# A hybrid trunk's first layer: exponentials moved to VectorE, a shorter parameter chain on GpSimd, and two steps moved forward in their queues

## The reference, cut to what matters

```
sh, sc, gt = split(silu(c) @ w_mod + b_mod, 3)          # the modulation
h = rms_norm(tokens, g) * (1 + sc) + sh                 # the prologue, for all 1280 tokens
u, v, g_a, xs, g_b = split(h @ w_in)                     # 5 parts of 512 columns
y_a = u * (w_s @ layer_norm(v) + b_s) * silu(g_a)        # chunked gMLP
dt  = exp(log_dt);  mag = exp(lam_re * dt)               # S5 discretization, 128 x 32 numbers
lb  = mag * (cos(lam_im * dt) + i sin(lam_im * dt))
f   = (lb - 1) / lam;   bb = f * b                       # then powers lb^1 .. lb^8
y_b = S5 scan of xs, both directions, from lb, bb, c     # then GELU, GLU, silu(g_b)
x   = x + gt * ([y_a, y_b] @ w_out)
```

## Time and profile before

| | us |
|---|---|
| median of 3 runs | 1297.3 |
| the profiled execution, own time | 1298.54 |
| its span | 1296.7 |
| TensorE busy, share of the span | 1221.9, 94% |
| VectorE / ScalarE / GpSimd busy | 814.5 / 518.7 / 499.6 |
| front: VectorE's `den` steps end | 11.3 |
| front: VectorE adds the squares, from | 12.2 |
| front: sums' input ready | 20.1 |
| front: norm refined (VectorE) | 24.7 |
| front: its rows spread and copied (ScalarE) | 27.1 |
| front: second modulation column block (TensorE) | 33.3 |
| front: first `v` operand complete (VectorE) | 35.6 |
| front: TensorE at the fourth modulation block | 48.4 |

### The profile page before, as it was taken

One profiled execution on the slowest core, in us unless ns is written; L12 is line 12 of the kernel. 1 busy time (PEld: TensorE's weight loads), 2 busy tenths in 40 slices (PEclk: granted clock), 3 DMA queues, 4 the chain that ended last, 5 costly groups with the idle time before them and its releaser, 6 DMA issues.

```text
span 1296.7 us, 20964 instructions
## 1 busy us (share of the span) xinstructions
PE 1221.9 (94%) x8450; PEld 1077.2 (83%) x8450; DVE 814.5 (63%) x1381; ACT 518.7 (40%) x968; POOL 499.6 (39%) x447
## 2 busy tenths in 40 slices
PE   3889899999999899999999999999999999999997
PEld 2888778887888849999999998877788888887997
DVE  4569647989916263146475899448876777765125
ACT  3633454220015331133524432147566666665012
POOL 5850000000000003331112112139999999998332
PEclk9998999999999899999999999999999999999998
DMA  9832677325431952113111122330000000000402
GB/s 336 318 106 91 171 216 247 131 87 200 168 107 61 333 216 86 34 42 135 53 34 34 33 74 82 106 98 9 9 17 9 17 11 15 17 9 9 163 29 103
DMA packets 89232, 130.09 MB, mean 100 GB/s; under 512 B 12944, under 2 KB 59408, under 8 KB 88336
## 3 DMA queue, kind: packets, MB, share of 16 engines
q1 hardware_dynamic: 79312, 113.96, 26.4%
q10 hardware_dynamic: 9824, 14.80, 3.4%
HBM read 97.81 MB, written 30.93 MB: 99 GB/s over the span
## 4 chain that ended last, share of the span: by engine, by line
PE 75%; DVE 7%; POOL 7%; DMA 6%; ACT 2%; issue 2%; SPq 1%; ACTq 0%; POOLq 0%; DVEq 0%
PE ps L1804 9%; PE ps L1806 9%; PE ps L1805 9%; PE ps L1815 5%; PE ps L1816 5%; PE ps L1817 5%; DVE region_d L1096 3%; PE ps L2063 3%; PE ps L2097 3%; PE ps L2098 3%; PE ps L2099 3%; POOL shared L553 3%; PE ps L2083 3%; PE ps L2086 3%; PE ps L2085 3%; PE ps L2084 2%
## 5 line engine op out<-in xcount | busy, mean ns | idle before, releaser
L1804 PE MATMUL ps<-w_hi,a_hi 128*128 128x256 f32 x896 | 257.2, 287 | 6.2 <-DVE b_lo L1152 2.4
L1805 PE MATMUL ps<-w_lo,a_hi 128*128 128x256 f32 x896 | 255.1, 285 | 0.0
L678 POOL TENSOR_TENSOR region_b<-region_b,region_d 128x256 f32<-128x256 f32 x40 | 29.8, 751 | 480.9 <-DVE region_d L1480 480.9
L1806 PE MATMUL ps<-w_hi,c_lo 128*128 128x256 f32 x736 | 209.2, 284 | 0.0
L1804 PEld LDWEIGHTS ps<-w_hi,a_hi 128*128 128x128 f32 x896 | 173.7, 194 | 9.0 <-issue 4.5
L1805 PEld LDWEIGHTS ps<-w_lo,a_hi 128*128 128x128 f32 x896 | 173.6, 194 | 0.0
L671 POOL TENSOR_TENSOR w_lo<-weight_ring,w_hi 128x2048 fp32r<-128x2048 f32 x16 | 74.1, 4631 | 200.1 <-ACT w_hi L726 200.1
L1576 DVE TENSOR_REDUCE small<-ps 128x1 f32<-128x1280 f32 x64 | 95.3, 1489 | 75.3 <-PE ps L2063 75.3
L1806 PEld LDWEIGHTS ps<-w_hi,c_lo 128*128 128x128 f32 x736 | 142.3, 193 | 0.0
L1815 PE MATMUL ps<-a_hi,w_hi 128*128 128x512 f32 (+1 forms) x384 | 138.0, 359 | 1.3 <-ACT region_d L726 1.3
L1816 PE MATMUL ps<-b_lo,w_hi 128*128 128x512 f32 (+1 forms) x384 | 136.0, 354 | 0.0
(11 more groups left out here) (234 smaller groups left out, 2940.4 us busy)
## 6 DMA issues: line engine op xcount, KB each, us to landing
weight_ring<-in_w_mod SPq DMA_DIRECT2D x10, 2048.0 KB, 9.2
weight_ring<-in_we_in SPq DMA_DIRECT2D x10, 1024.0 KB, 6.3
weight_ring<-in_wo_in SPq DMA_DIRECT2D x10, 1024.0 KB, 5.2
weight_ring<-cop_t_scratch SPq DMA_DIRECT2D x4, 1536.0 KB, 7.9
region_c<-in_w_mod SPq DMA_DIRECT2D x2, 2048.0 KB, 14.7
bop_scratch<-region_d ACTq DMA_DIRECT2D x16, 256.0 KB, 2.0
cop_t_scratch<-region_d SPq DMA_DIRECT2D x8, 512.0 KB, 7.5
weight_ring<-bop_scratch SPq DMA_DIRECT2D x2, 2048.0 KB, 10.4
```

What stands on the lines that cost most here:

```text
L1804: te.matmul(o, th, wh[:, k], start=first and k == 0, stop=False)
L1805: te.matmul(o, th, wl[:, k], start=False, stop=False)
L1806: last = te.matmul(o, tl, wh[:, k], start=False, stop=stop and k == KT - 1)
```

## The change

Four things are changed.

1. The two exponentials leave GpSimd. VectorE makes them with a new `exp_` of 16 steps, in which multiply and add are fused into `scalar_tensor_tensor`. The first stands right after `den`, before the squares are added; the second right after the squares are added, before the norm. The semaphore `s_exp` tells GpSimd of each; `s_den_ok` is gone.
2. GpSimd's chain starts at the angle, after the first exponential. It drops a copy, selects between sine and cosine with one difference instead of two masks, writes `lr` and `li` where the powers need them, and makes real and imaginary part of a power product in one operation of twice the width (four operations per doubling instead of six).
3. The first modulation block (`mods(0)`, `mod_cols(0)` on TensorE, `mod_row(0)` on ScalarE) stands ahead of the norm's sums. On ScalarE the rounding of the first `v` weights stands ahead of the copy of the norm's rows. The first four k now go through `gained`, `gained_round` and `gained_rest` like the others; for tokens 256 to 767 VectorE takes `gained` and `gained_rest` of one k in turn.
4. SyncE loads the second `xs` weights ahead of `cop_out(0)`.

```diff
@@ SyncE
+            ring_load("xs", 1)
             cop_out(0)
-            ring_load("xs", 1)
             kt_out(0)
@@ GpSimd
-            pool.wait_ge(s_ld_par, 16 * 3)
-            exp_(dt, ldt)
-            tt(xe, lamr, dt, ALU.mult)
-            exp_(mg, xe)
+            lr, li = LP[:, 1, 0], LP[:, 1, 1]
+            step(g.memset(LP[:, 0, 0], 1.0))
+            step(g.memset(LP[:, 0, 1], 0.0))
+            pool.wait_ge(s_exp, 1)
             tt(th, lami, dt, ALU.mult)
...
-            tt(sn, s_, even, ALU.mult)
-            tt(t1, c_, odd, ALU.mult)
-            tt(sn, sn, t1, ALU.add)
-            tt(cn, c_, even, ALU.mult)
-            tt(t1, s_, odd, ALU.mult)
-            tt(cn, cn, t1, ALU.add)
+            tt(t1, c_, s_, ALU.subtract)
+            tt(t1, t1, odd, ALU.mult)
+            tt(sn, s_, t1, ALU.add)
+            tt(cn, c_, t1, ALU.subtract)
             tt(sn, sn, sin_sign, ALU.mult)
             tt(cn, cn, cos_sign, ALU.mult)
+            pool.wait_ge(s_exp, 2)
...
             for m in (1, 2, 4):
...
+                A, O = LP[:, 1:m + 1], LP[:, m + 1:2 * m + 1]
+                M_ = [LP[:, m, r].unsqueeze(1).unsqueeze(1).broadcast_to([P, m, 2, G]) for r in range(2)]
+                tmp = ctmp[:, 0:2 * m * G].rearrange("p (m r g) -> p m r g", r=2, g=G)
+                tt(O, A, M_[0], ALU.mult)
+                tt(tmp, A, M_[1], ALU.mult)
+                tt(O[:, :, 0], O[:, :, 0], tmp[:, :, 1], ALU.subtract)
+                tt(O[:, :, 1], O[:, :, 1], tmp[:, :, 0], ALU.add)
@@ ScalarE
+            mod_row(0)
             act.wait_ge(s_ss_mm, 1)
             act.wait_ge(s_consts, 2)
             a.activation(rstd[:, 0:6], sums, ACT.Sqrt, bias=epsc, scale=1.0 / D).then_inc(s_rt, 1)
+            weights_round(("v", 0))
             act.wait_ge(s_bc_mm, 1)
             copy(rstd_rows[:, 0:T01], rows01).then_inc(s_bc_ok, 1)
-            weights_round(("v", 0))
-            mod_row(0)
             mod_row(1)
-            h_round(0)
-            h_round(1)
+            gained_round(0, range(4), 0)
+            gained_round(1, range(4), 4)
@@ VectorE
-            v.reciprocal(den, den).then_inc(s_den_ok, 1)
+            step(v.reciprocal(den, den))
+            def exp_(o, xin):
...
+                ts(x_, xin, -87.0, ALU.max, 88.0, ALU.min)
+                ts(k_, x_, 1.0 / math.log(2.0), ALU.mult, ROUND, ALU.add)
+                ts(k_, k_, -ROUND, ALU.add)
+                st(r_, k_, -LN2_HI, x_, ALU.mult, ALU.add)
+                st(r_, k_, -LN2_LO, r_, ALU.mult, ALU.add)
+                ts(e_, r_, 1.0 / 5040, ALU.mult)
+                for q in (720.0, 120.0, 24.0, 6.0, 2.0, 1.0):
+                    st(e_, e_, 1.0 / q, r_, ALU.add, ALU.mult)
+                ts(k_, k_, 127.0, ALU.add, 2.0 ** 23, ALU.mult)
+                cp(p_, k_)
+                st(e_, e_, 1.0, p_.bitcast(F32), ALU.add, ALU.mult)
+                v.scalar_tensor_tensor(out=o, in0=xin, scalar=-87.0, in1=e_, op0=ALU.is_ge, op1=ALU.mult).then_inc(s_exp, 1)
+            exp_(dt, ldt)
+            dve.wait_ge(s_exp, 1)
+            tt(xe, lamr, dt, ALU.mult)
...
             v.tensor_tensor(XQ[:, 0, 0:T01], XQ[:, 0, 0:T01], XQ[:, 4, 0:T01], ALU.add).then_inc(s_pre, 1)
+            exp_(mg, xe)
...
-            scaled(0)
-            scaled(1)
             weights_rest(("v", 0))
+            dve.wait_ge(s_bc_ok, 1)
             half_evac(0)
-            h_rest(0)
-            h_rest(1)
+            gained(0, range(4))
+            gained_rest(0, range(4), 0)
+            for k in range(4):
+                gained(1, (k,))
+                gained_rest(1, (k,), 4 + k)
@@ TensorE
+            mods(0)
+            mod_cols(0)
             pe.wait_ge(s_pre, 1)
             for t in range(6):
                 last = te.matmul(sums[:, t:t + 1], XQ[:, 0, P * t:P * t + P], onec, start=True, stop=True)
             last.then_inc(s_ss_mm, 1)
             rstd_across(0)
-            mods(0)
-            mod_cols(0)
             mods(1)
```

More of the change, by code:

```diff
@@ L258, in build @@
             sem("mod_mm"), sem("mod_ok"), sem("sq"), sem("rt_req"), sem("rt_ok"))
[L259 to L260 removed]
+        s_pre, s_bc_mm, s_bc_ok, s_v_mm, s_v_ev, s_ss_mm, s_z2 = (
+            sem("pre"), sem("bc_mm"), sem("bc_ok"), sem("v_mm"), sem("v_ev"), sem("ss_mm"), sem("z2"))
         s_vn_ok, s_vg_ok, s_bl_ok, s_bl_tr, s_bl_ev, s_cl_ok = (
@@ L559, in cp @@
                 step(g.tensor_copy(o, a))
[L561 to L578, removed]
             def halved(o, xin):
@@ L598, in _ @@
             ts(kf, kf, -ROUND, ALU.add)
-            cp(rr, th)
-            for q in PIO2:
+            for i, q in enumerate(PIO2):
                 ts(t1, kf, -q, ALU.mult)
-                tt(rr, rr, t1, ALU.add)
+                tt(rr, rr if i else th, t1, ALU.add)
             tt(r2, rr, rr, ALU.mult)
@@ L608, in _ @@
             tt(s_, s_, rr, ALU.mult)
+            ts(c_, r2, -1.0 / 3628800, ALU.mult, 1.0 / 40320, ALU.add)
+            for q in (-1.0 / 720, 1.0 / 24, -0.5, 1.0):
+                tt(c_, c_, r2, ALU.mult)
+                ts(c_, c_, q, ALU.add)
             halved(t1, kf)
             low_bit(odd, kf, t1)
-            ts(even, odd, -1.0, ALU.mult, 1.0, ALU.add)
             tt(t2, t1, odd, ALU.add)
@@ L640, in _ @@
             tt(fi, t1, den, ALU.mult)
[L641 to L644, removed]
             for m in (1, 2, 4):
[L646 to L650, removed]
-                tt(tmp, A[1], M_[1], ALU.mult)
-                tt(O[0], O[0], tmp, ALU.subtract)
-                tt(O[1], A[0], M_[1], ALU.mult)
-                tt(tmp, A[1], M_[0], ALU.mult)
-                tt(O[1], O[1], tmp, ALU.add)
+                A, O = LP[:, 1:m + 1], LP[:, m + 1:2 * m + 1]
[5 more added lines that the diff above has]
+                tt(O[:, :, 1], O[:, :, 1], tmp[:, :, 0], ALU.add)
             fwd, bwd = slice(0, NS), slice(NS, P)
@@ L852, in _ @@
             a.activation(rstd[:, 6:TT], ssq[:, 6:TT], ACT.Sqrt, bias=epsc, scale=1.0 / D).then_inc(s_rt, 1)
-            gained_round(0, range(4, KT), 0)
-            gained_round(1, range(4, KT), 4)
+            gained_round(0, range(4, KT), 8)
+            gained_round(1, range(4, KT), 12)
             act.wait_ge(s_bc_mm, 2)
             copy(rstd_rows[:, T01:TOK], ps[:, 7, :]).then_inc(s_bc_ok, 1)
-            gained_round(2, range(KT), 8)
+            gained_round(2, range(KT), 16)
             for t in range(TT):
@@ L1123, in _, with st @@
             tt(den, den, fr, ALU.add)
-            v.reciprocal(den, den).then_inc(s_den_ok, 1)
+            step(v.reciprocal(den, den))
+            def exp_(o, xin):
+                x_, k_, r_, e_ = (vjunk[:, 32 * i:32 * i + 32] for i in range(4))
+                p_ = vjunk[:, 128:160].bitcast(I32)
+                def st(o, a, s1, b, op0, op1):
+                    step(v.scalar_tensor_tensor(out=o, in0=a, scalar=s1, in1=b, op0=op0, op1=op1))
+                ts(x_, xin, -87.0, ALU.max, 88.0, ALU.min)
[13 more added lines that the diff above has]
+            tt(xe, lamr, dt, ALU.mult)
             def weights_rest(u):
@@ L1143, in half_evac @@
                 dve.wait_ge(s_mod_ok, e + 1)
-            def h_rest(q):
-                t0, nt = CHUNKS[q]
-                ci = 1 if q == 0 else 0
-                for k in range(4):
-                    dve.wait_ge(s_h_hi, 4 * q + k + 1)
-                    z = hT0[:, k, t0:t0 + nt]
-                    v.tensor_tensor(h_lo[:, k, t0:t0 + nt], z, hi[:, k, t0:t0 + nt].bitcast(F32), ALU.subtract).then_inc(s_h_lod, 1)
             def gained(q, ks):
```

28 lines of the change are left out of this document (3 added, 25 removed).

## The result

The changed kernel took 1285.43 us (median of four runs, 1283.55 to 1288.34) against 1297.3: 0.9905 of before, interval 0.989 to 0.9919. That is 3.4 us above the forecast of 1282 and inside its range. The profiled execution took 1286.58 with a span of 1284.8; before it was 1298.54 and 1296.7. So the spans differ by 11.9 us where the sum had 15.7, and the 3.8 us between are the subject here. The span is the profiled execution's own extent, 1.8 us shorter than its time.

What follows compares the result with a forecast made beforehand. Bound: TensorE, busy 94%, its gaps caused by GpSimd's parameter chain, then VectorE's in-order work. Front 0.3, gaps 2.9 + 2.5 + 5.4 and slow clock 4.7 made 15.8 us, taken as 15.7: 1282, range 1277 to 1289.

Steps and rivals of the forecast that it cites:

- rival F: GpSimd's parameter chain ends no earlier; the moved load alone gives 5.4 us, so 1292; chance 0.02.
- gap 3: TensorE's wait of 5.68 us at 162.37 for C-operator tiles, released by VectorE; forecast to shrink to 0.3.
- one of its own signs of being wrong: TensorE's clock still falling would show it wrong; forecast was no low-clock stretch between 90 and 180 us.
- Rival E: GpSimd's parameter chain still rules, deciding from 0.93 us a step; 1311 at 1.1 us a step; chance 0.03.
- I give the front 0.3 us: From 0 to 75 us: gain of 0.3 us, between -3 and +2, with VectorE free at 74.5.
- Rival C: Front late by contention of the exponentials or the in-turn chunk: up to 3 us lost, 1285; chance 0.11.
- The cost of the move on SyncE is one issue: Moved xs load on SyncE: one issue of 0.4 us ahead of four stores that wait anyway, so it costs nothing.
- its gap of 1.38 stays: TensorE's second lag block: its gap of 1.38 us with no releaser was expected to remain.
- without the slow clock: TensorE's stretches at the lower clock after its gaps were expected to go, worth 4.7 us, 2.0 in the second lag block.
- Rival B: TensorE's gaps go but the slow clock stays: 1286; chance 0.12.
- After that nothing is tied to the absolute time: Behind the second lag block, weights, stores and operator loads follow events moved by 15 to 16 us, keeping the gain.
- rival D: Past 150 us SyncE's stores bring back 3 to 6 us of gap 3: 1286 to 1288; chance 0.10.

Runs made afterwards that it cites:

- e2: The kernel before with only the load of the second xs weights moved ahead of cop_out(0): 1293.89 us, 0.9952.
- e1: The changed kernel with the second xs weights loaded after cop_out(0) again: 1292.72 us, 0.9954.
- e4: The changed kernel with GpSimd's power products held until VectorE has finished the 256-token rest of the last four k: 1292.76 us, 0.9947.
- e5: The changed kernel with SyncE waiting for the second four B-operator stores before loading the second xs weights: 1287.86 us, 0.9917.
- after_again: The changed kernel run once more, nothing altered: 1286.67 us, 0.991.
- e3: The changed kernel with part 3 of the change (the new order of the front) undone, exponentials still on VectorE: 1287.72 us, 0.9907.
- e10: The changed kernel with the second lag block cut around xs tile 8, last bop transposes after tile 9, u_in(2) at j == 11: 1288.8 us, 0.9927.
- e12: e10 with ScalarE's load u_in(2) moved behind the last xs store: 1287.86 us, 0.9925.
- the third: The changed kernel run again, nothing altered, on the same chip as e10: 1288.29 us, 0.9923.

## Why the prediction was right, and where 3.8 us went

**Right.** GpSimd's chain ended at 58.5 (46 to 68 forecast, 56 at the old mean step), BB follows VectorE's own work, the load goes out at 108.66 (108), the three gaps sum to 0.85, and CL(0) and CL(1) come at 117.86 and 149.59 for 116.9 and 148.6, both 1.0 late. e2 confirms rival F's price for the load alone (1292; its profiled span is 4.7 below that of before, for 5.4), and e1 that it carries gap 3. But one of its own signs of being wrong came: the clock still fell, between 159 and 163 us. And the last `xs` store went out at 187.16 for 183. The time is inside the range although the front, the gap and the clock are all off to the same side, by 3.8 us together. Rival E is out: a step took 43.6/81 = 0.54 us, far from its 0.93. Its nearest trace is the start, three steps in 4.47 us beside VectorE's long additions.

**Step 1 of the difference: the front, 1.0 us.** "I give the front 0.3 us" failed: VectorE ends at 75.5, where 74.5 was forecast and the kernel before had 74.8. Rival C had the place and the wrong cause: not the exponentials (16 steps in 3.7 us, 0.23 each, as priced) but the double-width power products and copies, which before met VectorE only while it stood waiting. e4 shows it. The 256-wide groups are 1.8 us longer, and 0.85 of that lies over a wait for ScalarE (1.44 before, 0.59 now): 0.95 remains. This holds for the execution profiled first. In five of the nine profiles these groups start at 53.9 to 54.5 us instead of 52.6, their length is spent where VectorE otherwise waited for ScalarE, and it is the late start, whose cause stays open, that makes BB 1.2 to 1.9 us late.

The path through the front was not the one I told either. TensorE never reached the fourth modulation block 2 us earlier (48.25 for 48.42). It led by 1.45 us at the first `v` operand and was 0.15 behind at the third modulation block (39.65 for 39.50): the lower clock from 33 to 40 us had taken the lead, not the transfer that lands at 53. The in-turn chunk would have taken it as well: ScalarE's copy of the modulation row stands behind that chunk and ends at 43.63, and TensorE waits 0.49 us for it at 43.68.

**Step 2: ScalarE's queue behind the load, 0.25 us.** "The cost of the move on SyncE is one issue" held for SyncE. The transfers beside it were not in the sum, and gap 3 came 12.55 us early for 13.8, 0.25 more than step 1 explains. That split is a remainder. Followed along the path, TensorE comes to the first lag block at 118.64 for 118.0, 0.65 late by the front; e5 puts 0.4 on the delayed store; 0.2 of the 1.25 stays unassigned.

**Step 3: "its gap of 1.38 stays", 0.9 us.** It is 2.27, and 1.47 to 3.66 in the other profiles that have it. It ends with the instruction packet, not with anything of the kernel's data, and was taken for a constant.

**Step 4: "without the slow clock", 1.65 us**, the remainder, and 1.6 by the comparison with after_again. The clock fell behind exactly this gap. Rival B had it stay although the gaps went; here it came back behind a gap that I had left standing, and not each time: with 1.91 (e2), 2.27, 2.78 (e4), 3.45 (e5) and 3.66 us it fell, with 2.61 and 1.78 (after_again, e3) it did not, nor with 1.38 (before) and 1.47 (e1), where a stretch at the lower clock had just ended. The price of that stretch was off as well: the block without its gap took 6.1 us (149.82 to 158.20 less 2.27), not 5.7, so the slow clock in it had cost 1.6 and not 2.0. The remainder hides these 0.4, because the end gains 0.2 over the gMLP and the sum's rounding 0.1.

15.7 - 1.0 - 0.25 - 0.9 - 1.65 = 11.9, the difference of the spans. Steps 1 to 3 are sums of rows of one execution, 2 and 4 are remainders. The split holds for this execution alone; after_again has the larger gap without step 4.

**A step that would have failed anyway.** "After that nothing is tied to the absolute time" passed only because the gain was smaller. In the changed kernel TensorE's lead goes through the B-operator stage whole (11.7 us at the gMLP, 11.6 at 219.53). With 2.8 us more (e10) all but 0.4 of it was lost in that stage; with 2.45 more (e12) all of it, a part of that by the clock. With a lead of 15.7 us, 4 beyond the changed kernel's, rival D would likely have taken the rest. Whether by the bytes of the loads or, as I had it, by SyncE's issues, is open: in both variants SyncE issued the load late for TensorE's new lead, and in e12 it also took 3 us longer to land. That 15.7 itself would be cut is argued from these two, not run.

No variant beats the changed kernel by more than the runs can tell apart.

## What to carry to other kernels

When a bound engine is freed, look at what the faster engine now runs beside: the same wide GpSimd operations cost nothing next to a waiting VectorE and lengthen a working one's by 14 to 67%. A gap without a releaser is not a constant of the sum: here it lay in a dense run of short matmuls and ended with a packet of instructions, and the clock could fall behind it. Before adding up gaps, read the DMA share of the stage that comes after them, and when its loads are issued: they bound how much of the lead can pass. And when two profiles meet at one point, ask whether they came there by the same path: e3 did not.

## What the runs showed of the hardware

- GpSimd operations of 128x256 and 64x512 lengthen VectorE's two-input operations: 256-wide from 0.42 to 0.70 us each, 512-wide from 0.68 up to 0.96 (groups of four, divided by four). GpSimd's own 64x512 copies take 0.66 us while VectorE waits (before), 0.72 partly beside 256-wide ones and 1.00 beside 512-wide ones (e4). GpSimd steps of 32 elements leave VectorE's at 0.68 but come every 0.65 us, in place of 0.38 with the hand-over the earlier trace rows.
- A store issued 1.2 us behind a 1 MB load held its buffer for 5.5 us (109.88 to 115.39). With that load held back (e5), ScalarE's longest wait for it was 1.05 us.
- The granted clock fell after a gap of 2.27 us and not after one of 2.61, in the same kernel. A stretch at the lower level is worth 1.6 us here, nearly all of the 1.7 us between these two executions; the third differs by more, through its front and its gap.
- In nine profiles TensorE's gap without a releaser, 1.38 to 3.66 us long, ends 2.3 to 2.5 us after the start of a 16 KB packet of instructions.
